# Down projections by seven block products instead of eight, in three feed-forward stages

## The reference

```python
h = h + jnp.square(jax.nn.relu(z @ w_up[l])) @ w_down[l]          # "mlp", hidden width 4096
...
def swiglu(x, w_in, w_out):                                       # "ffn1" and "ffn2", hidden width 2816
    gate, up = jnp.split(x @ w_in, 2, axis=-1)
    return (jax.nn.silu(gate) * up) @ w_out
...
x = x + 0.5 * rms_norm_2(swiglu(h, ffn1_w_in[l], ffn1_w_out[l]), ffn1_post_g[l])
```

## Time and profile before

| | us |
|---|---|
| median of 3 runs (2884.46 to 2887.8) | 2885.11 |
| the profiled execution's own time | 2884.54 |
| its span, first to last instruction | 2882.7 |
| PE busy | 2853.4 |
| DVE busy | 1680.7 |
| ACT busy | 1172.4 |
| POOL busy | 486.0 |
| bytes read and written in HBM | 257.03 and 75.24 MB |

### The profile page before, as it was taken

One profiled execution on the slowest core, in us unless ns is written; L12 is line 12 of the kernel. 1 busy time (PEld: TensorE's weight loads), 2 busy tenths in 40 slices (PEclk: granted clock), 3 DMA queues, 4 the chain that ended last, 5 costly groups with the idle time before them and its releaser, 6 DMA issues.

```text
span 2882.7 us, 35432 instructions
## 1 busy us (share of the span) xinstructions
PE 2853.4 (99%) x13496; PEld 2344.2 (81%) x13496; DVE 1680.7 (58%) x2487; ACT 1172.4 (41%) x1861; POOL 486.0 (17%) x1023
## 2 busy tenths in 40 slices
PE   8999999999999999999999999999999999999999
PEld 7788888888887888888888878887788888888887
DVE  6754866543444478777754463336647866665354
ACT  6524555432233365333333343136645433333332
POOL 0000000010000000789988300011100000000000
PEclk9999999999999999999999999999999999999999
DMA  3123233274442132233345632212124222224443
GB/s 136 44 94 118 103 117 110 99 266 145 150 144 96 58 110 74 90 129 109 120 162 184 231 136 77 85 66 77 62 83 159 74 88 81 78 84 171 163 150 137
DMA packets 100745, 335.77 MB, mean 116 GB/s; under 512 B 12400, under 2 KB 13168, under 8 KB 98272
## 3 DMA queue, kind: packets, MB, share of 16 engines
q1 hardware_dynamic: 82512, 260.08, 26.1%
q0 software_dynamic: 18064, 73.41, 6.9%
HBM read 257.03 MB, written 75.24 MB: 115 GB/s over the span
## 4 chain that ended last, share of the span: by engine, by line
PE 96%; DVE 2%; ACT 1%; DMA 1%; issue 0%; SPq 0%; DVEq 0%; ACTq 0%
PE ps L127 29%; PE ps L129 29%; PE ps L128 29%; PE ps L2332 1%; PE ps L2347 1%; PE ps L2306 1%; PE ps L275 1%; PE ps L346 0%; PE ps L1982 0%; PE ps L1033 0%; DMA weight_sums<-hid 0%; PE ps L2015 0%; PE ps L2023 0%; DVE acc L186 0%; PE ps L1995 0%
## 5 line engine op out<-in xcount | busy, mean ns | idle before, releaser
L127 PE MATMUL ps<-ring_b 128*128 128x512 f32 x832 | 324.8, 390 | 1.8 <-DVE ring_b L1269 1.8
L129 PE MATMUL ps<-ring_b 128*128 128x512 f32 x832 | 323.8, 389 | 0.0
L128 PE MATMUL ps<-ring_b 128*128 128x512 f32 x832 | 323.7, 389 | 0.0
L888 ACT ACTIVATE up_slots<-weight_sums 128x512 fp32r<-128x512 f32 x216 | 136.3, 632 | 313.0 <-PE ps L129 292.6
L127 PE MATMUL ps<-region_a,up_slots 128*128 128x512 f32 x640 | 250.0, 391 | 0.0
L129 PE MATMUL ps<-region_a,up_slots 128*128 128x512 f32 x640 | 249.1, 389 | 0.0
L128 PE MATMUL ps<-region_a,up_slots 128*128 128x512 f32 x640 | 249.1, 389 | 0.0
L127 PEld LDWEIGHTS ps<-ring_b 128*128 128x128 f32 x832 | 156.2, 188 | 35.1 <-DVE ring_b L1269 2.6
L127 PE MATMUL ps<-region_a,region_b 128*128 128x512 f32 x448 | 180.8, 403 | 3.4 <-DVE region_b L122 2.4
L129 PEld LDWEIGHTS ps<-ring_b 128*128 128x128 f32 x832 | 156.2, 188 | 32.5
L128 PEld LDWEIGHTS ps<-ring_b 128*128 128x128 f32 x832 | 156.2, 188 | 32.1
(11 more groups left out here) (446 smaller groups left out, 6435.9 us busy)
## 6 DMA issues: line engine op xcount, KB each, us to landing
raw<-feed SPq DMA_DIRECT2D x212, 512.0 KB, 3.6
raw<-stream SPq DMA_DIRECT2D x56, 512.0 KB, 3.5
weight_sums<-hid SPq DMA_DIRECT2D x94, 256.0 KB, 3.8
far_raw_b<-feed SPq DMA_DIRECT2D x38, 512.0 KB, 4.4
x_mid<-acc POOLq DMA_DIRECT2D x32, 512.0 KB, 3.2
hid_raw<-hid SPq DMA_DIRECT2D x58, 256.0 KB, 3.8
hid<-late_pieces SPq DMA_DIRECT2D x27, 512.0 KB, 2.6
ssm_row<-ssm_mid POOLq DMA_DIRECT2D x8, 1632.0 KB, 7.5
```

What stands on the lines that cost most here:

```text
L127: nc.tensor.matmul(psum, lhs(0), rhs(0), start=first, stop=False)
L128: nc.tensor.matmul(psum, lhs(0), rhs(1), start=False, stop=False)
L129: return nc.tensor.matmul(psum, lhs(1), rhs(0), start=False, stop=last)
L888: nc.scalar.activation(up_slot(F, i)[:, 0, :], F.weight(p, q), ACT.Copy).then_inc(F.sem["hi"], 1)
```

## The change

The down product is seen as 2x2 blocks: the hidden rows in pairs of blocks (`F.m` = `F.n` / 2 pairs `kp`), the output in two row halves and two column halves. Strassen's first form makes seven products of sums of blocks. They are laid in four groups over all pairs, `F.S` = 4 `F.m` steps: groups 0, 1 and 3 hold two products (24 matmuls per step), group 2 one (12 per step). The third product of a triple is as before.

The five sums of activations per pair (`hid_sum_dve`) are made by DVE in the up stage; two of them overwrite a block that is no longer needed. `hid` now holds seven blocks of 128x512 per pair instead of four, and `store` waits for the sums. The sums of weights (`row_sum_dve`) are made on the way, one step before the split: two in groups 0 and 1, none in group 2, one in group 3. Per step SP loads 1280 KB in groups 0 and 1 (a row of weights, half a row more, two blocks of `hid`), 512 KB in group 2 and 1 MB in group 3, into three places in turn; four slots hold the split operands. At a group's end the PSUM banks are joined into the accumulator in SBUF by DVE, in groups 0 and 1 also copied by ACT; the last group is joined tile by tile (`tile_half_dve`, `tile_sum_dve`). In mlp the old rows, which stood in the accumulator, are loaded elsewhere and added in group 2 (`old_row_dve`). `FAR_K` becomes 3. Slots, raw rows and small buffers get other places, and some loads of units, `gb` and old rows wait for other events. The hooks of the next norm start at step 3 `F.m` + 1, and in ffn1 the first ones also wait for POOL's tables (`s_out`).

Core of the diff (lines taken out are mostly left out here):

```diff
-        NEAR_K, FAR_K = 2, 4
-        HID_NEAR, ROWS_FROM = 6, 8
+        NEAR_K, FAR_K = 2, 3
...
+            def down_bank(self, g, a, i):
+                if g < 2:
+                    return ([4, 5, 6, 7] + [self.bank_at(j) for j in range(self.N - 4, self.N)])[2 * i + a]
+                return (4, 5, 2, 3)[i] if g == 2 else self.tile_bank(i) + a
+            def down_bank_free(self, g, a, i):
+                bank = self.down_bank(g, a, i)
+                if g == 0:
+                    return [self.emptied(j) for j in range(self.N - 4, self.N) if self.bank_at(j) == bank]
+                if g == 1:
+                    return [self.tile_joined(i + 1) if a else self.tile_copied(2 * i + 1)]
+                for i0 in range(4):
+                    if g == 3 and self.down_bank(2, 0, i0) == bank:
+                        return [self.at("sum", i0 + 1)]
+                for i0 in range(4):
+                    for a0 in range(2):
+                        if self.down_bank(1, a0, i0) == bank:
+                            return [self.tile_joined(4 + 2 * i0 + 1 + a0)]
...
+            def slot_key(self, s):
+                return 0 if s == 0 else {1: 1, 2: 2, 3: 0, 0: 3}[s % 4]
+            def down_slot(self, s):
+                key = self.slot_key(s)
+                return self.main_slot if key == 3 else self.zx[:, key]
+            def down_slot_free(self, s):
+                if s < 3:
+                    return self.at("done", self.N - 4 + s)
+                if s == 4:
+                    return self.ended()
+                return self.down_done([x for x in range(s) if self.slot_key(x) == self.slot_key(s)][-1])
...
+        def hid_sum_dve(dve, F, kp, name):
+            one, two, op, dst = {"m6": ((0, 0), (0, 1), ALU.subtract, F.extra(0)),
+                                 "m2": ((0, 0), (1, 0), ALU.add, F.extra(1)),
+                                 "m1": ((0, 1), (1, 0), ALU.add, F.block(kp, 0, 0)),
+                                 "m5": ((0, 1), (1, 1), ALU.add, F.extra(0 if F.gated else 2)),
+                                 "m7": ((1, 1), (1, 0), ALU.subtract, F.block(kp, 1, 1))}[name]
+            for u, th in (one, two):
+                dve.wait_ge(*F.block_made(kp, u, th))
+            if name == "m1":
+                dve.wait_ge(*F.hid_summed(kp, "m6"))
+                dve.wait_ge(*F.hid_summed(kp, "m2"))
+            elif name == "m7":
+                dve.wait_ge(*F.hid_summed(kp, "m5"))
+            elif not F.gated:
+                dve.wait_ge(*F.at("kept_e", 16 * kp))
+            elif name == "m2":
+                dve.wait_ge(*F.at("kept_e1", 16 * kp))
+            else:
+                dve.wait_ge(*F.at("kept_e", 32 * kp + (16 if name == "m5" else 0)))
+            nc.vector.tensor_tensor(dst, F.block(kp, *one), F.block(kp, *two), op).then_inc(F.sem["hid_sum"], 1)
...
+                for kp, name in F.sums_at(i):
+                    hid_sum_dve(dve, F, kp, name)
+                if i >= F.N - 3:
+                    down_lo(dve, F, i - F.N + 3)
+                if i >= F.N - 4:
+                    row_sum_dve(dve, F, i - F.N + 4)
...
+        def down_hi(act, F, s):
+            slot, g = F.down_slot(s), F.group(s)[0]
+            act.wait_ge(*F.down_slot_free(s))
+            act.wait_ge(*F.rows_in(s))
+            if g == 2:
+                nc.scalar.activation(slot[:, 0, 0, :], F.hid_row(s)[:, 0:HALF], ACT.Copy).then_inc(F.sem["hi"], 1)
+                nc.scalar.activation(slot[:, 2, 0, :], F.weight_row(s)[:, 0:HALF], ACT.Copy).then_inc(F.sem["hi"], 1)
             else:
+                nc.scalar.activation(slot[:, 0:2, 0, :], halves(F.hid_row(s)), ACT.Copy).then_inc(F.sem["hi"], 1)
+                act.wait_ge(*F.row_summed(F.row_sums(s)))
+                nc.scalar.activation(slot[:, 2:4, 0, :], halves(F.weight_row(s)), ACT.Copy).then_inc(F.sem["hi"], 1)
+        def row_sum_dve(dve, F, s):
+            g, w, more = F.group(s)[0], F.weight_row(s), F.more_row(s)
+            near, far = w[:, 0:HALF], w[:, HALF:]
+            if g == 2:
+                return
+            dve.wait_ge(*F.rows_in(s))
+            if g == 0:
+                nc.vector.tensor_tensor(near, near, more, ALU.add).then_inc(F.sem["sums"], 1)
+                nc.vector.tensor_tensor(far, far, more, ALU.subtract).then_inc(F.sem["sums"], 1)
+            elif g == 1:
+                nc.vector.tensor_tensor(far, far, near, ALU.add).then_inc(F.sem["sums"], 1)
+                dve.wait_ge(*F.row_summed(F.row_sums(s) - 1))
+                nc.vector.tensor_tensor(near, more, near, ALU.subtract).then_inc(F.sem["sums"], 1)
+            else:
+                nc.vector.tensor_tensor(near, near, far, ALU.add).then_inc(F.sem["sums"], 1)
+        def down_lo(dve, F, s):
+            slot, g = F.down_slot(s), F.group(s)[0]
+            for x, row in enumerate((F.hid_row(s), F.weight_row(s))):
+                dve.wait_ge(*F.at("hi", F.N + 2 * s + x + 1))
+                if g == 2:
+                    nc.vector.tensor_tensor(slot[:, 2 * x, 1, :], row[:, 0:HALF], slot[:, 2 * x, 0, :].bitcast(f32),
+                                            ALU.subtract).then_inc(F.sem["lo"], 1)
+                else:
+                    nc.vector.tensor_tensor(slot[:, 2 * x:2 * x + 2, 1, :], halves(row),
+                                            slot[:, 2 * x:2 * x + 2, 0, :].bitcast(f32),
+                                            ALU.subtract).then_inc(F.sem["lo"], 1)
+        def down_products(F, g, a, i, s, first, last):
+            slot = F.down_slot(s)
+            of_hid, of_weight = ([(0, 2), (1, 3)], [(0, 3), (1, 2)], [(0, 2)], [(0, 2), (1, 3)])[g][a]
+            return products(ps[:, F.down_bank(g, a, i), :], lambda h: slot[:, of_hid, h, i * P:(i + 1) * P],
+                            lambda h: slot[:, of_weight, h, :], first, last)
...
+        def down_join_dve(dve, F, g, i):
+            c11, c21, c22 = acc[:, 4 + i, 0:HALF], acc[:, i, 0:HALF], acc[:, i, HALF:]
+            dve.wait_ge(*F.tile_done(g, i))
+            if g == 0:
+                dve.wait_ge(*F.tile_copied(2 * i + 2))
+                nc.vector.tensor_tensor(c22, c11, ps[:, F.down_bank(0, 1, i), :], ALU.add).then_inc(F.sem["joined"], 1)
+            elif g == 1:
+                dve.wait_ge(*F.tile_joined(4))
+                nc.vector.tensor_tensor(c22, c22, ps[:, F.down_bank(1, 0, i), :], ALU.add).then_inc(F.sem["joined"], 1)
+                dve.wait_ge(*F.tile_copied(8 + i + 1))
+                nc.vector.tensor_tensor(c11, c11, ps[:, F.down_bank(1, 1, i), :], ALU.add).then_inc(F.sem["joined"], 1)
+            else:
+                dve.wait_ge(*F.tile_joined(12 + i))
+                if not F.gated:
+                    dve.wait_ge(*F.old_added())
+                nc.vector.tensor_tensor(c21, c21, ps[:, F.down_bank(2, 0, i), :], ALU.add).then_inc(F.sem["joined"], 1)
+                dve.wait_ge(*F.tile_joined(12 + i + 1))
+                nc.vector.tensor_tensor(c22, c22, ps[:, F.down_bank(2, 0, i), :], ALU.subtract).then_inc(F.sem["sum"], 1)
...
+        def tile_half_dve(dve, F, t):
+            bank = F.down_bank(3, 1, t - 4)
+            dve.wait_ge(*F.tile_half(t - 4))
+            nc.vector.tensor_tensor(acc[:, t, 0:HALF], acc[:, t, 0:HALF], ps[:, bank, :], ALU.subtract).then_inc(F.sem["joined"], 1)
+            nc.vector.tensor_tensor(acc[:, t, HALF:], acc[:, t, HALF:], ps[:, bank, :], ALU.add).then_inc(F.sem["joined"], 1)
...
+                if g < 3 and k == F.m - 1:
+                    down_join_dve(dve, F, g, 2)
+                    down_join_dve(dve, F, g, 3)
+                if s + AHEAD_DOWN < F.S:
+                    down_lo(dve, F, s + AHEAD_DOWN)
+                if s + AHEAD_DOWN + 1 < F.S:
+                    row_sum_dve(dve, F, s + AHEAD_DOWN + 1)
+                if g < 3 and k == F.m - 2:
+                    down_join_dve(dve, F, g, 0)
+                    down_join_dve(dve, F, g, 1)
+                if not F.gated and g == 2 and 2 <= k < 2 + NT:
+                    old_row_dve(dve, F, k - 2)
...
+            def down(s):
+                g, kp = F.group(s)
+                if s == 0:
                     sp.wait_ge(*F.raw_read(F.pairs - 2))
+                    sp.wait_ge(*F.at("done", F.N - 6))
+                elif s < 3:
+                    sp.wait_ge(*F.at("done", F.N - (4, 1)[s - 1]))
+                elif s == 3:
+                    sp.wait_ge(*F.at("lo", F.N))
                 else:
+                    sp.wait_ge(*F.row_read(s - 3))
+                    if s == 5:
+                        for cond in F.all_stored():
+                            sp.wait_ge(*cond)
+                if g == 0 and s != 5:
+                    for cond in F.all_stored(kp):
                         sp.wait_ge(*cond)
+                got = F.sem[("raw0", "raw1", "rows")[s % 3]]
+                rows = [F.feed[2 * F.pairs + 2 * kp + r, :, :] for r in range(2)]
```

(63 more changed lines are left out.)

448 lines of the change are left out of this document (252 added, 196 removed).

## The result

Measured side by side with the kernel before, the changed kernel takes **2857.4 us** (median of 4 runs, 2856.1 to 2857.9) against 2885.6 us: a ratio of 0.9901, 95% interval 0.9883 to 0.9918. It is 28.3 us faster. The forecast was 2817 us with a range from 2784 to 2852: the direction was right, the time 40 us too low and outside the range.

What follows compares the result with a forecast made beforehand. PE (TensorE), busy 2853.4 of 2882.7 us, was taken as the bound. 2884.5 - 103.4 + 28 - 3 + 5 + 2 + 3 = 2816.1, forecast as 2817 us, range 2784 to 2852.

Steps and rivals of the forecast that it cites:

- Matmuls removed: Down stages: 456 products go at 0.2267 us each, 103.4 us less, with nothing hiding it.
- Up to down: Turns from up to down stage: new PE waits, 9 us per gated stage and 10 in mlp, +28 us (0 to 60).
- burst: Steps 5 to 7 of a down stage: gains and old rows share the DMA engines with row loads, 3.7 us.
- The -3 for the waits of before: Down stages: of the 3.9 us PE already waited on down operands, 3 us go.
- POOL in ffn1: ffn1's down stage: POOL's tables end 33 us later beside two-operand DVE work, old rows late, +3 us (0 to 25).
- Group to group: Between down groups: PE waits for banks that pass through DVE, 1.7 us in each of three stages, +5 us (0 to 9).
- tails: Tails behind mlp and ffn1: more DVE sums per tile and tiles following sooner, +2 us (-1 to 5).
- Steady steps and up stages: Inside down groups and in up stages: DVE's added sums and the larger loads stay hidden, cost 0.
- Rival B: ffn1: tables end 67 us late, old rows cost +20 us, first groups drift 10 us more: 2847 us, 15%.
- Rival C: Wide groups and the fourth: loads become the bound, steps last 7.0 us, slower than before at 2960 us; 4%.

Runs made afterwards that it cites:

- e1: Changed kernel with POOL's six table operations in ffn1 replaced by two memsets: 2842.1 us.
- experiments 2, 4 and 8: Changed kernel: mlp and ffn2 old rows later, 2851.2 us; turn reordered, 2850.1; both plus earlier tables, and step 4's loads ahead of last stores, 2818.3.
- experiment 1: POOL's table operations in ffn1 replaced by memsets, in the changed kernel (2842.1 us) and, as control, in the kernel before (2888.5 us).
- experiment 7: Changed kernel with ffn1's added sums replaced by memsets of the same places (2848.8 us), then by memsets mostly one element wide (2840.8 us).
- the last kernel: Changed kernel with six order edits, the last putting DVE's joins first at the third group's end: 2810.5 us, ratio 0.9736 to the kernel before.
- experiment 3: Kernel before, with idle DVE sums added ahead of four splits in ffn2's down stage so that PE waits: 2914.9 us.
- e11: Changed kernel with turn, table and late-row reorderings, step 4's loads ahead of stores, and ffn1's gains and old rows issued between POOL's last tables: 2814.8 us.
- e4: Kernel before, with 12, 14, 17 and 22 idle DVE sums ahead of four ffn2 down splits: 2914.9 us.

## Why the prediction was wrong

By its own steps:

- **Matmuls removed, -103.4.** Right: 13496 - 13040 = 456, at the same pitch in the steady steps.
- **Up to down, +28.** Right in sum and mostly in mechanism: 10.7 us in mlp, 8.8 in ffn1, 10.6 in ffn2, 30.1 together. In ffn2 the join wait was 2.27 us and ended 7.2 us after the up stage, as worked out; in ffn1 and mlp it was 3.78 and 3.08. That the sum fits is in part luck. I counted 3.7 us of burst in ffn1 too, although by my own section on POOL its old rows stand behind the tables; steps 5 to 7 had no wait there, and the join wait and step 4's (4.11 us for 2.8) made up for it. In e1, where the rows do come early, the burst cost ffn1 3.8 us. What I took for a price of the change was mostly order, on DVE, SP and POOL: experiments 2, 4 and 8 brought the 30.1 us down to 2.9. The -3 for the waits of before came as counted.
- **POOL in ffn1, +3.** Mis-sized. The tables came 61 us late, not 33. The two waits behind them are 8.3 us, not 3, with 4.6 us of slower products behind; the time without tables was 15.3 us less (experiment 1). I priced 67 us of two-operand work at a half. The half was fair (experiment 7), but the work was 102 us, as the trace prints the durations: 68 of sums and 34 of splits. That made 53 us of delay; 2.5 us more waiting for stores and a start 6 us later relative to the down stage make up the 61.
- The Trainium skill, "SBUF — State Buffer", section "Who interferes with whom", has a VectorE instruction with two SBUF inputs hold the port that GpSimd's reads need for its whole length. By it I had worked out 67 us of lateness and 20 us of time; the runs gave 61 and 15. That is near by chance: held up for the whole of each such instruction, POOL would have lost 102 us, and it lost 53. This need not contradict the rule, since POOL does not read in every moment; no run here shows that. That memsets, which read nothing, cost far less than sums agrees with what the section says of reads; that they still delay the tables by 6 us does not follow from it, and one execution each does not settle it.
- **Group to group, +5, and tails, +2.** The joins between groups cost 2.5 us. The tails were mis-sized: PE is idle 6.7 us in mlp's against 3.1 before (884 to 1026 us) and 9.4 us behind ffn1's down stage against 5.7, so 7.4 us more where I had 2 and at most 5, and some 2.5 us more in ffn2's last steps, which I had not priced. The waits are for DVE (4.15 us at 912.0, 3.23 at 1708.6); no run takes them apart, and they stand in the last kernel too (4.14 us at 903.1, 3.23 at 1679.6).
- **Steady steps and up stages, 0.** Right for the down steps. The up stages last 1.3, 2.6 and 1.0 us longer: 5 us that I had at nothing, 2.1 of them in waits under 1 us and 1.7 in slower products at ffn1's start.
- **The clock: the step that failed.** Every wait was priced at its length. PE's idle time rose by 49.8 us where I had 35; the other 26.2 us of the miss are PE's busy time, and 16.7 of these are products at half the clock behind waits. The forecast had no such term, and the earlier trace rows could not show its price: the trace of the kernel before stands at the full clock from 10 us to 2880 us, behind waits of 2.47 and 2.08 us too. That such a loss comes behind longer waits is shown in experiment 3, without the change.

The sum: 2816.1 + 14.8 + 26.2 = 2857.1, the profiled execution's own time. The 14.8 us are +2.1 at the turns, -2.5 between groups, +5.3 behind the tables, +7.9 in the tails, +2.1 in the up stages and -0.1 elsewhere. Rival B had the right mechanism in ffn1 (waits behind late tables) and a near time, 2847, but counted 10 us of drift that did not come. Rival C is out: at steady demand nothing waited for loads (1520 to 1560 us: PE busy 40.00 of 40.00 us with the DMA engines at 0.79).

What stays open: what makes the tails longer, why the price of two-operand work to POOL is a half, and behind which of the waits the clock falls.

## What to carry to other kernels

When work is taken from a saturated engine, the gain is collected only as far as the chain stays unbroken: price a new wait at its length and, from about 2 us on, at 1.5 to 3 us of slower matmuls that may come behind it. At the turn from one stage to the next, write out for each queue what stands ahead of the first loads of the next stage; a store that waits for a result, placed before a load that waits for nothing, was worth 14 us here. And an engine that ran 43 us ahead of need (POOL's last table at 1605.0 in the kernel before, the first use of the rows behind it at 1648.0) is part of the critical path as soon as the change both slows it and calls for it sooner.

## What the runs showed of the hardware

The clock does not follow a wait's length alone. The same wait of mlp's turn stands in the changed kernel and in the one with earlier tables, which differ only some 600 us later. PE in the changed kernel:

```profile
584.37 0.50 PE L127 MATMUL ps<-mixed_b 128*128 128x512 f32 x1 [3.08 <-DVE pieces_b L1153]
...
585.17 0.40 PE L127 MATMUL ps<-mixed_b 128*128 128x512 f32 x1
585.40 0.39 PE L128 MATMUL ps<-mixed_b 128*128 128x512 f32 x1
585.63 0.39 PE L129 MATMUL ps<-mixed_b 128*128 128x512 f32 x1
```

And with the tables earlier:

```profile
584.08 0.50 PE L127 MATMUL ps<-mixed_b 128*128 128x512 f32 x1 [3.07 <-DVE pieces_b L1153]
...
585.22 0.63 PE L128 MATMUL ps<-mixed_b 128*128 128x512 f32 x1
585.65 0.63 PE L129 MATMUL ps<-mixed_b 128*128 128x512 f32 x1
586.08 0.63 PE L127 MATMUL ps<-mixed_b 128*128 128x512 f32 x1
```

One runs on at 0.23 us per product, the other falls to 0.43 us, about 1 us after PE has begun again, and loses 1.7 us. A wait of 2.08 us ahead of ffn1's up stage, which both kernels have, cost nothing more before the change and 1.7 us after it; the clock fell behind it in ten of the eleven traces of kernels with the change and in none of the three without, and what makes the difference stays open. The shortest wait between 128x512 products with a fall close behind it is 1.82 us (e11, at 1502.7); that of 1.64 us in e4 had none. So such a loss can be given a size but no certainty, and two executions of one kernel could differ by it.
